# Three more projections of the first block as seven half-size products, with their weight sums on VectorE

## The reference

```python
h = rmsnorm(x, attn_norm_w[l])
z = h @ w_in[l]
hq, hf, hi, hg, cq, ckv, kr, gate_a, gate_b = jnp.split(z, split_idx, axis=-1)
o_a = hgrn2_mixer(hq, hf, hi, hg, lb_all[l], hg_out_norm_w[l]).astype(x.dtype)
o_b = mla_mixer(cq, ckv, kr, positions, mla_q_norm_w[l], mla_w_uq[l], ...)
y = jax.nn.sigmoid(gate_a) * (o_a @ w_branch_hgrn[l]) + jax.nn.sigmoid(gate_b) * (o_b @ w_branch_mla[l])
```

## Time and profile before

| | us |
|---|---|
| median of 3 runs | 1583.83 |
| lowest, highest | 1582.14, 1585.29 |
| the profiled execution's own time | 1583.95 |
| its span in the trace | 1582.2 |
| TensorE matmul busy | 1262.6 |
| VectorE busy | 552.8 |
| ScalarE busy | 201.4 |

### The profile page before, as it was taken

One profiled execution on the slowest core, in us unless ns is written; L12 is line 12 of the kernel. 1 busy time (PEld: TensorE's weight loads), 2 busy tenths in 40 slices (PEclk: granted clock), 3 DMA queues, 4 the chain that ended last, 5 costly groups with the idle time before them and its releaser, 6 DMA issues.

```text
span 1582.2 us, 20568 instructions
## 1 busy us (share of the span) xinstructions
PE 1262.6 (80%) x9054; PEld 797.0 (50%) x9054; DVE 552.8 (35%) x943; ACT 201.4 (13%) x413; POOL 0.5 (0%) x5
## 2 busy tenths in 40 slices
PE   9999999999756846756656665675676999999998
PEld 8967988854313412212212221221221488999985
DVE  5788666732000100101001010010010497798522
ACT  1102033020000000000000000000000211135411
POOL 0000000000000000000000000000000000000000
PEclk9999999999978968878878878877878999999999
DMA  9443165589999999999999999999999654434240
GB/s 365 156 164 130 65 220 226 208 356 426 438 431 436 427 436 437 433 429 441 431 432 436 431 439 432 432 439 431 432 437 425 286 213 159 161 113 167 108 160 27
DMA packets 20565, 507.00 MB, mean 320 GB/s; under 512 B 4240, under 2 KB 4368, under 8 KB 6544
## 3 DMA queue, kind: packets, MB, share of 16 engines
q1 hardware_dynamic: 20208, 505.70, 76.5%
q10 hardware_dynamic: 288, 0.26, 0.0%
HBM read 504.91 MB, written 1.05 MB: 320 GB/s over the span
## 4 chain that ended last, share of the span: by engine, by line
PE 54%; DMA 40%; DVE 5%; issue 1%; ACT 0%; SPq 0%; DVEq 0%; ACTq 0%
DMA ring<-in_experts 37%; PE psP L1317 12%; PE psP L1370 11%; PE psP L753 10%; PE psP L1368 6%; PE psP L801 4%; DMA arena<-in_experts 2%; PE psA L816 2%; DVE arena L1981 2%; PE psP L1477 1%; PE psB L1694 1%; DVE ring L1981 1%; PE psB L1303 1%; PE psA L732 1%; PE psP L1417 0%
## 5 line engine op out<-in xcount | busy, mean ns | idle before, releaser
L1981 DVE TENSOR_TENSOR X<-X,psA 128x512 f32<-128x512 f32 x66 | 45.3, 687 | 695.2 <-PE psA L816 681.0
L753 PE MATMUL psP<-arena 128*32 128x512 f32 x1024 | 150.4, 740 | 133.9 <-DMA arena<-in_experts 133.8
L753 PE MATMUL psP<-ring,arena 128*32 128x512 f32 x1024 | 150.7, 742 | 131.7 <-DMA ring<-in_experts 131.7
L753 PEld LDWEIGHTS psP<-ring,arena 128*32 128x32 f32 x1024 | 38.2, 132 | 239.6 <-issue 235.8
L753 PEld LDWEIGHTS psP<-arena 128*32 128x32 f32 x1024 | 35.9, 132 | 242.2 <-DMA arena<-in_experts 123.5
L1370 PE MATMUL psP<-arena,ring 128*128 128x128 f32 x944 | 111.4, 276 | 1.9 <-DVE ring L1981 1.9
L1370 PEld LDWEIGHTS psP<-arena,ring 128*128 128x128 f32 x944 | 108.1, 192 | 3.4 <-DVE ring L1981 2.5
L1317 PE MATMUL psP<-ring,arena 128*128 128x512 f32 (+2 forms) x240 | 85.9, 515 | 0.0
L801 PE MATMUL psP<-arena 128*32 128x512 f32 x512 | 66.5, 678 | 19.1 <-DMA arena<-in_experts 17.7
L801 PE MATMUL psP<-ring,arena 128*32 128x512 f32 x512 | 65.5, 663 | 19.3 <-DMA ring<-in_experts 17.9
L1981 DVE TENSOR_TENSOR arena<-arena 128x1024 f32<-128x1024 f32 (+6 forms) x103 | 79.2, 798 | 1.5
(11 more groups left out here) (349 smaller groups left out, 1381.4 us busy)
## 6 DMA issues: line engine op xcount, KB each, us to landing
arena<-in_experts SPq DMA_DIRECT2D x7, 4096.0 KB, 21.3
ring<-in_experts SPq DMA_DIRECT2D x7, 4096.0 KB, 22.9
ring<-in_u_gl SPq DMA_DIRECT2D x6, 2048.0 KB, 8.2
ring<-in_u_hq SPq DMA_DIRECT2D x2, 2048.0 KB, 23.4
ring<-in_u_hv SPq DMA_DIRECT2D x2, 2048.0 KB, 11.2
ring<-in_u_hg SPq DMA_DIRECT2D x2, 2048.0 KB, 8.8
ring<-in_u_ga SPq DMA_DIRECT2D x2, 2048.0 KB, 8.7
ring<-in_u_gb SPq DMA_DIRECT2D x2, 2048.0 KB, 8.7
```

What stands on the lines that cost most here:

```text
L753: mm = pe.matmul(z[j * CAP:(j + 1) * CAP, :], x[:, 4 * half + k, j * CAP:(j + 1) * CAP], held[c % 4][:, k // 2, j, (k % 2) * 512:(k % 2 + ...
L1981: return dve.tensor_tensor(o, a, b, op)
```

## The change

`cl`, `hg1` and `ga1` join `FIRST`, and so are made in seven products; `cl` and `hg1` are token-major. Their sums are put in: those of `cl` between the sums of `hv1` and the `late` of `hv0`; those of `hg1` before `ch`; those of `ga1` before `ga0` (after `cnorm`). `gb0`'s and `gb1`'s stay before `ga1` and `gb0`. Buffers are dealt out anew: `cl` has area 9 for its own, the others take turns at `w_spare` and `w_10`.

```diff
-FIRST = ["hq0", "hq1", "hv0", "hv1", "hg0", "ga0", "gb0", "gb1", "wa0", "wa1", "wb0", "wb1"]
+FIRST = ["hq0", "hq1", "hv0", "hv1", "cl", "hg0", "hg1", "ga0", "ga1", "gb0", "gb1", "wa0", "wa1", "wb0", "wb1"]
...
-BY_TOKENS = {"hv0", "hv1", "hg0", "dq", "dv", "dk", "mv", "mq", "mk"}
+BY_TOKENS = {"hv0", "hv1", "cl", "hg0", "hg1", "dq", "dv", "dk", "mv", "mq", "mk"}
...
     sums("hv1")
+    sums("cl")
     late("hv0")
     proj("hv0")
     p.append(("level", 0, "AB"))
-    before = {"cl": "hg0", "hg1": "ga0", "ga1": "gb0", "gb0": "gb1"}
+    before = {"cl": "hg0", "ch": "hg1", "hg1": "ga0", "ga0": "ga1", "ga1": "gb0", "gb0": "gb1"}
...
-        w_10, w_7, w_8 = ([area(a, 4, 256, off=1024 * i) for i in range(2)] for a in (10, 7, 8))
+        w_9, w_10, w_7, w_8 = ([area(a, 4, 256, off=1024 * i) for i in range(2)] for a in (9, 10, 7, 8))
...
-        first_sums = {"hq0": w_spare, "hq1": w_10, "hv0": w_spare, "hv1": w_10, "hg0": w_spare, "ga0": w_10,
-                      "gb0": w_spare, "gb1": w_apart,
+        first_sums = {"hq0": w_spare, "hq1": w_10, "hv0": w_spare, "hv1": w_10, "cl": w_9, "hg0": w_spare, "hg1": w_10,
+                      "ga0": w_spare, "ga1": w_10, "gb0": w_spare, "gb1": w_apart,
...
-            return {"dv": dv, "mv": mv}.get(arg, rope_in)
+            return {"dv": dv, "mv": mv, "cl": C}.get(arg, rope_in)
...
-            last_used = {"hv0": "hq0", "hv1": "hq1", "hg0": "hv0", "ga0": "hv1", "gb0": "hg0", "wb0": "wa0", "wb1": "wa1"}
+            last_used = {"hv0": "hq0", "hv1": "hq1", "hg0": "hv0", "hg1": "hv1", "ga0": "hg0", "ga1": "hg1", "gb0": "ga0", "wb0": "wa0", "wb1": "wa1"}
```

## The result

The change makes the kernel slower: in the first comparison 1590.70 us median (1589.01 to 1591.82, 6 runs) against 1582.64 (1582.14 to 1585.29, 6 runs), ratio 1.0048 with a 95% interval of 1.0037 to 1.0058. A second comparison gave 1590.07 (1589.48 to 1590.77, 5 runs) against 1582.98 (18 runs), 1.0046 (1.0032 to 1.0060). The forecast was 1588.8, in a range of 1584.8 to 1591.6.

What follows compares the result with a forecast made beforehand. VectorE was to become the bound between level 0 and level 8: -5.18 us on TensorE and +10.1 of waits make +4.9 on 1583.95, so 1588.8 us, range 1584.8 to 1591.6 (own range 1587 to 1590).

Steps and rivals of the forecast that it cites:

- VectorE's queue as the bound: Between level 0 and level 8, 18.5 us of added work make VectorE the bound instead of TensorE.
- Some 110 of 115.5 us: Sign that the forecast is right: VectorE's busy time between level 0 and level 8.
- The steps: Level-by-level chain from level 0 to level 8, each step set by VectorE's fixed order; level 8 begins at about 189.7.
- The rule of 7.17 + 3.53 + 4.06: VectorE's copies and multiplications, a later unit's sums, and `late` to next copy: a full step takes 14.76 us.
- Level 0: The sums of `cl` delay `hv0`'s `late` by 3.53 us; level 0 begins at 74.19 instead of 72.89, +1.30.
- `ga0` the dearest step: `ga1`'s sums stand ahead of `ga0`'s `late`; level 6 begins 5.35 us later, TensorE idle for nearly 4 us.
- The sum: -5.18 us on TensorE, +10.1 of waits at product 4 and level 3's masked copy: +4.9 us.
- its rival with a chance of 0.20: The clock halves behind `ga0`'s 3.98 us wait at product 4, costing 1.67 us: +6.6, 1590.5; chance 0.20.
- One of the signs that were to show the forecast wrong: A granted clock under 1.00 around 158 us.
- The argument against it: Against a halved clock at `ga0`: TensorE never idle for long here; the stretch with the 1.33 us wait ran at 1.00.
- The rival of the gain: Between level 0 and level 8 TensorE stays the bound and all 5.18 us are kept, 1578.8; chance 0.09.
- Nothing given back behind level 8: `gb1` and all after it, with the experts' stream, are as before; nothing gives the lost 4.9 us back.

Runs made afterwards that it cites:

- the sums cut: The changed kernel with the sums of `cl`, `hg1` and `ga1` made over 8 of 256 columns only; 1580.06 us, ratio 0.9983 to the kernel before.
- the wait filled: The changed kernel with 14 idle products put on TensorE ahead of its wait for `ga0`'s late sum; 1588.37 us, ratio 1.0034 to the kernel before.
- `ga1` alone: The kernel before with only `ga1` made in seven products, its sums ahead of `ga0`'s late sum; 1589.13 us, ratio 1.0036.
- the change with the memsets moved: The changed kernel with level 0's two memsets (`hattn`, `suf`) moved ahead of `hq0`'s late sum; 1588.36 us, ratio 1.0029 to the kernel before.
- the single edits: The kernel before with only `cl`, only `hg1` or only `ga1` made in seven products; 1583.94, 1583.68 and 1589.13 us, ratios 1.0006, 1.0003 and 1.0036.
- `cl` alone: The kernel before with only `cl` made in seven products; 1583.94 us, ratio 1.0006.
- the GpSimd kernel: The changed kernel with the four sums each of `cl`, `hg1` and `ga1` on GpSimd; 1591.92 us, ratio 1.0054 to the kernel before.

## Why the prediction was right, and where not

- **VectorE's queue as the bound.** Right, and shown: with the sums cut, 9.5 us go (2.1 of them the clock), and with `ga1`'s sums moved into a wait of VectorE's, their cost vanishes. "Some 110 of 115.5 us" busy were 109.94 of 117.70.
- **The steps.** The rule of 7.17 + 3.53 + 4.06 held to a few hundredths. Lengths between level starts 0-1, 1-2, 4-5 were forecast as 15.14, 14.76, 14.76 and are 15.14, 14.77, 14.71 in the first profile after; 2-4 was 21.93 and is 21.91. The whole was 115.48 and is 115.61 once the clock is out. The one step that was off is 5-6, forecast as 19.10 and 19.28 with the wait filled: the prediction gave `ga0`'s five products ahead of the transposes 8.94 us, where the kernel before has 9.13 (140.02 to 149.15).
- **Level 0.** +1.30 us was right, and measured as 1.3. The words beside it are not: 1.30 is not "most of the 3.53", and TensorE had been the later one by 2.2 us, not "by little".
- **`ga0` the dearest step, with nearly 4 us of wait.** Right: 3.98, the forecast's figure.
- **The sum is where it failed.** The forecast was +4.9. By the medians and the ratios it is +7.6 to +8.1 in the first comparison and +7.1 to +7.3 in the second, outside the forecast's own range of 1587 to 1590 (1590.70 and 1590.07). The term that the prediction had left out of its sum is the clock behind that wait, its rival with a chance of 0.20 and 1.67 us, and 1590.5 is where the rival had put the time. One of the signs that were to show the forecast wrong, a granted clock under 1.00 around 158, did come. The clock fell in both profiles of the change and in that of `ga1` alone, at 1.6 to 2.1 us. With it the sum is 6.5 to 7.0. That the wide range held the result is owed to its making room for this rival. The argument against it, that TensorE was never idle for long ahead of the wait, did not hold: all three waits of 3.98 us that weren't filled in these two kernels, and the fourth in the change with the memsets moved, lowered the clock.
- **What is left of the 7.56 us** of the first pair of profiles, behind 4.9 and 2.1 for the clock, is 0.13 from the steps and 0.44 from level 0, late by 1.74 instead of 1.30; the first products of TensorE ended at 15.05 us there and at 14.62 before, so this lies ahead of the change. A median against a median leaves half a microsecond more in the first comparison, which no profile pins down.
- **The rival of the gain**, "TensorE stays the bound", is excluded by the single edits, of which none is faster. The Trainium skill, "Perfetto Trace Analysis", "Identifying the Most-Contended Engine", has the engine of highest occupancy eased first. By matmul busy time that is TensorE, 109.88 against 92.00, and the measurement goes against easing it at this price: the change put 17.94 us on VectorE and took 5.18 off TensorE. The same section says that for TensorE matmul busy time doesn't tell how near the engine is to its limit, and names the busy share of the weight loads beside another measure; the weight loads are busy for 87.02 us here, less than VectorE. The prediction left this half of the section out.
- **Nothing given back behind level 8.** Right for the first pair of profiles: 7.56 there, 7.7 at the end. In the second profile of the change 1.2 us more than before lie behind level 8, among the experts, and whether the change has a part in that is open, since `cl` alone has 2.2 and the first profile 0.1.

## What to carry to other kernels

Before work is moved from a busy engine to one with free time, count that free time in the stretch and at the places where it lies: a sum put where its engine waits anyway is free, one put a step later, in front of something that another engine waits for, costs its length and perhaps the clock (`ga1`'s three sums, 5.17 us of length between their two places). In an engine's fixed queue nothing should stand ahead of an urgent instruction that is first needed a step later. And a recurrence of a few measured lengths (this queue's work per step, the other engine's per step, the larger of the two) forecast this pipeline to 0.13 of 115.6 us, the clock apart.

## What the runs showed of the hardware

- The granted clock fell to 0.50, the lower level of 1.2 GHz, at all four unfilled waits of 3.98 us, in a stretch where TensorE was otherwise busy. It also fell at a wait of 2.19 us (product 4 of 2.88 instead of 2.05), and in the GpSimd kernel behind waits of 6.57 and 2.82 us, though behind 2.96 us among the experts it hadn't. The length of a wait alone doesn't decide it.
- The Trainium skill's "TensorE: Matmul & The Clock Gate", "HAM oscillation — how this bites in real kernels", warns of idle gaps. The traces agree for those of 3.98 us; by its rule the gap of 2.19 us would be harmless, and there the measurement decides.
- Fourteen small products in the wait kept the clock, at a net gain of 1.7 us (1588.37 against 1590.07 in the same comparison).
- Beside a GpSimd sum of two SBUF operands, VectorE's took 3.38 us instead of 1.22, and GpSimd's 3.34 instead of 2.35: the two hardly overlap, as 1.22 + 2.35 = 3.57.
- The same kernel's level 0 began at 74.63 and at 72.48 in two executions, and the time behind level 8 was 1397.6 and 1398.6 us; compare lengths between two points of a profile, not starts or whole times.
